# State space layer over quads of tokens: two groups on the halves of the array, tables made in the preceding block, states as stationary operand

## The reference

```
    lb_re, lb_im = mag * jnp.cos(ang), mag * jnp.sin(ang)          # one complex factor per group and state
    bb_re = cr[..., None] * b_re - ci[..., None] * b_im
    bb_im = cr[..., None] * b_im + ci[..., None] * b_re
    bu_re = jnp.einsum('blgh,gph->blgp', u, bb_re)
    bu_im = jnp.einsum('blgh,gph->blgp', u, bb_im)
    ...
    _, _, s_re, s_im = lax.associative_scan(combine, (a_re, a_im, bu_re, bu_im), axis=1)
    y = (jnp.einsum('ghp,blgp->blgh', c_re, s_re) - jnp.einsum('ghp,blgp->blgh', c_im, s_im)
         + d_skip.reshape(S5_GROUPS, S5_GROUP) * u)
    y = jax.nn.gelu(y.reshape(b_, L, D_MODEL), approximate=False)
    val, gate = jnp.split(y @ w_glu, 2, axis=-1)
    return val * jax.nn.sigmoid(gate)
```

## Time and profile before

| | us |
|---|---|
| median of 3 runs | 3628.16 |
| lowest and highest | 3626.93, 3628.58 |
| span of the profiled execution | 3628.5 |
| PE busy in it | 3462.6 |
| DVE busy | 2325.0 |
| ACT busy | 1840.1 |
| POOL busy | 509.8 |

### The profile page before, as it was taken

How to read it: one execution, slowest core, us unless ns; L and a number is a source line. 1 busy time by engine, 2 the same in 40 slices (tenths; PEclk the granted TensorE clock), 3 DMA queues, 4 the chain that set the end, 5 groups by cost and what they waited for, 6 DMA issues and landing times.

```text
span 3628.5 us, 63324 instructions
## 1 busy us (share of the span) xinstructions
PE 3462.6 (95%) x21770; PEld 3025.4 (83%) x21770; DVE 2325.0 (64%) x3755; ACT 1840.1 (51%) x2784; POOL 509.8 (14%) x546
## 2 busy tenths in 40 slices
PE   9997999999999999989999999999479999999998
PEld 7885888888888888878888888888468788888887
DVE  5687665555555766775765565778975665565566
ACT  4477454545454655544554454554554554454443
POOL 0001310111114000214000001133022000000105
PEclk9998999999999999999999999998589999999999
DMA  6561545555555555535455555652035455555555
GB/s 213 169 191 41 185 156 189 185 192 185 190 185 191 168 189 170 161 120 167 148 189 187 183 190 192 197 191 95 25 111 186 139 196 191 185 188 188 185 186 190
DMA packets 176036, 615.99 MB, mean 170 GB/s; under 512 B 19030, under 2 KB 28312, under 8 KB 175656
## 3 DMA queue, kind: packets, MB, share of 16 engines
q1 hardware_dynamic: 173212, 609.35, 51.9%
q10 hardware_dynamic: 2700, 4.96, 0.5%
HBM read 611.35 MB, written 2.88 MB: 169 GB/s over the span
## 4 chain that ended last, share of the span: by engine, by line
PE 88%; DVE 8%; ACT 2%; issue 1%; DMA 1%; SPq 0%; POOL 0%; ACTq 0%; DVEq 0%; POOLq 0%
PE bank L1881 53%; PE bank L1884 28%; PE m L1904 2%; DVE prod L1664 1%; DVE w_lo L1012 1%; DVE st L1667 1%; DVE st L1669 1%; PE m L1906 1%; PE m L1894 1%; ACT w_hi L433 0%; DVE y L1039 0%; PE m L2396 0%; PE bank L2396 0%; PE m L2297 0%; DVE res L1045 0%
## 5 line engine op out<-in xcount | busy, mean ns | idle before, releaser
L1012 DVE TENSOR_TENSOR w_lo<-w_raw,w_hi 128x1024 fp32r<-128x1024 f32 x1086 | 1336.2, 1252 | 815.6 <-ACT w_hi L433 809.6
L1881 PE MATMUL bank<-act,w_hi 128*128 128x512 f32 x6016 | 1512.6, 393 | 8.6 <-DVE w_lo L1012 7.9
L433 ACT ACTIVATE w_hi<-w_raw 128x1024 fp32r<-128x1024 f32 x1090 | 1130.1, 1055 | 389.8 <-PE bank L1884 348.9
L1881 PEld LDWEIGHTS bank<-act,w_hi 128*128 128x128 f32 x6016 | 1082.3, 189 | 209.0 <-DVE w_lo L1012 8.9
L1884 PEld LDWEIGHTS bank<-act,w_lo 128*128 128x128 f32 x6016 | 821.4, 191 | 58.9
L1884 PE MATMUL bank<-act,w_lo 128*128 128x256 f32 x6016 | 839.4, 282 | 0.0
L1881 PE MATMUL bank<-ffn,w_hi 128*128 128x512 f32 x2432 | 613.6, 393 | 1.3 <-DVE w_lo L1016 1.0
L442 ACT ACTIVATE low<-bank 128x256 f32<-128x256 f32 x542 | 207.9, 384 | 781.5 <-PE bank L1884 780.7
L1881 PEld LDWEIGHTS bank<-ffn,w_hi 128*128 128x128 f32 x2432 | 436.3, 189 | 79.5 <-DVE w_lo L1016 1.2
L1020 DVE TENSOR_TENSOR ev<-bank,low 128x256 f32<-128x256 f32 x468 | 198.3, 424 | 249.5 <-ACT low L442 243.5
L1884 PEld LDWEIGHTS bank<-ffn,w_lo 128*128 128x128 f32 x2432 | 333.9, 190 | 25.2
(11 more groups left out here) (412 smaller groups left out, 2490.3 us busy)
## 6 DMA issues: line engine op xcount, KB each, us to landing
w_raw<-stream SPq DMA_DIRECT2D x1148, 512.0 KB, 3.4
bias<-toeplitz SPq DMA_DIRECT2D x4, 512.0 KB, 9.0
out<-res SPq DMA_DIRECT2D x3, 512.0 KB, 2.9
res<-x_t SPq DMA_DIRECT2D x2, 512.0 KB, 9.0
res<-x_t ACTq DMA_DIRECT2D x2, 512.0 KB, 11.0
bias<-toeplitz SPq DMA_DIRECT2D x4, 256.0 KB, 11.8
b_raw<-s_b ACTq DMA_DIRECT2D x1, 1024.0 KB, 5.4
c_raw<-s_c ACTq DMA_DIRECT2D x1, 1024.0 KB, 4.7
```

Source lines behind the costliest of these rows:

```text
L433: a(w_hi[:, q, :], w_raw[:, q, :], ACT.Copy).then_inc(hi_ready, 1)
L1012: e.tensor_tensor(w_lo[:, q, :], w_raw[:, q, :], w_hi[:, q, :].bitcast(F32), ALU.subtract).then_inc(lo_ready, 1)
L1881: mm(bank[w][:, 0:2 * n], w_hi[:, q, wt], x(h * hk + k, 0, 2 * n), start=(h == 0 and k == 0), stop=False)
```

## The change

The stage works on four tokens at a time (quads). In words:

- **Recurrence.** The state after every fourth token is kept: 62 steps instead of 127 for each half of the groups, by the factor's fourth power. The step is unchanged (three instructions of the same shapes), `SKEW` is 12.
- **Layout of u.** Of every group the 16 channels of four tokens stand on 64 partitions, two groups on the two halves of the array. ACT writes the gained residual to `u_own`; PE moves it to that layout by 64 products with a 0/1 matrix `placing` (K = 32, 128 columns of weights, 256 columns of tokens read at every fourth; float32), partly between the sums of squares; DVE scales eight 128x512 tiles from PSUM to `u_quad` by the reciprocal root, which is now 64 columns wide.
- **Inputs.** 256 matmuls of 64x64 weights and 64 columns, two at a time on opposite quarters of the array; 16 PSUM tiles, 14 copied by ACT, 2 by DVE.
- **Tables.** C times five powers (`cd`, 48 DVE steps over 128x640) behind the up and down units of group 1, B times four powers (`b_lhs`, 16 times two steps over 128x512 and two over 128x256) behind group 2, with 16 loads of B and 16 of the powers (256 KB each) that ACT issues. PE does 6 transposes in group 0 in place of 32 in group 2. The 256 products for the direct taps, L2371, go from before the norm to the time of the scan (L2407). The down phase of group 0 is now written out on all engines, on ACT and DVE group 1 too.
- **Direct taps.** `k_own` is copied out of PSUM on 16 rows a half; eight SBUF-to-SBUF DMAs from SP place it, shifted, in `k_rhs` (runs of at most 256 bytes, 6144 of them in six DMAs, and two DMAs of whole rows); 128 matmuls multiply it, during the scan.
- **States.** `turned` becomes the stationary operand, `cd` the moving one (256 matmuls of 64x64, 64 columns); `gelu`; then 128 more matmuls with the identity turn the result back, the last two of eight tiles inside `first_pair` of `glu`. The rows of `w_glu` are permuted to suit.
- **Weights of glu.** `st` is half as large, so `hi` and `lo` of the first `glu` pair stand before the scan, and SP loads the second pair then.

The diff, cut to its core:

```diff
-    SKEW = 16
+    SKEW = 12
+    QUADS = 64
+    BY_DVE = (5, 7)
...
+    SLOT_UP1, SLOT_DOWN1, SLOT_UP2, SLOT_DOWN2 = 16, 48, 64, 88
+    C_SLOTS = [16 + n if n < 24 else 43 + n - 24 if n < 29 else 48 + (n - 29) * 16 // 19 for n in range(48)]
+    B_SLOTS = [66 + 11 * k // 4 if k < 8 else 88 + 2 * (k - 8) for k in range(DT)]
...
+        for half in range(2):
+            for j in range(4):
+                src, to = slice(64 * half, 64 * half + 16), slice(64 * half + 16 * j, 64 * half + 16 * j + 16)
+                sp_eng.dma_start(k_rhs[to, :, 16 * j:64], k_own[src, :, 0:64 - 16 * j]).then_inc(sem("k_moved"), 16)
...
+            if step == 0:
+                chain(e.tensor_tensor(to, table(0), c_of(r), ALU.mult))
+            elif step == 1:
+                chain(e.tensor_tensor(c_part[:, :, :, :], table(1), c_of(1 - r), ALU.mult))
...
+            for n in range(8):
+                h, i = n // 4, n % 4
+                v.wait_ge(sem("u_placed"), n + 1)
+                e.tensor_tensor(u_quad[:, 32 * h + i:32 * h + 32:4, :], five[n][:, :].rearrange("p (k c) -> p k c", k=8),
+                                rstd_row[:, :].unsqueeze(1).to_broadcast([P, 8, 64]), ALU.mult).then_inc(sem("u_scaled"), 1)
+            g0 = PH["glu"][0]
+            for q in range(4):
+                lo(g0, q)
...
-            for c in range(1, 128 + SKEW):
+            steps_ = QUADS - 1
+            for c in range(1, steps_ + SKEW):
...
+            def place(h, quad, of, done):
+                for j in range(4):
+                    for i in of:
+                        src, k0 = slice(32 * i, 32 * i + 32), 8 * h + 4 * quad
+                        last = mm(five[4 * h + i][:, 256 * quad:256 * quad + 256], placing[src, P * j:P * j + P],
+                                  u_own[src, k0:k0 + 4, j:T:4], start=(j == 0), stop=(j == 3))
+            for k in range(DT):
+                if k % 4 == 0 and k:
+                    place((k - 4) // 8, (k - 4) // 4 % 2, range(4) if k <= 8 else (0, 1), k == 8)
+                last = mm(m[5][:, 0:T], ones[:, :], u5_sq[:, k, :], start=(k == 0), stop=(k == DT - 1))
+            last.then_inc(sum_spread, 1)
+            place(1, 1, (0, 1), True)
+            pe.wait_ge(root_taken, NORM["s5"] + 1)
+            for i in (2, 3):
+                for quad in range(2):
+                    place(1, quad, (i,), quad == 1)
...
+            def states(n):
+                for k in range(8):
+                    for r in range(2):
+                        for rows in half_rows:
+                            last = mm(five[n][rows, 64 * k:64 * k + 64], turned[n][rows, k, r, :],
+                                      cd[rows, r, 8 * n + k, 1:5, :].rearrange("p d f -> p (d f)"), start=False, stop=(k == 7 and r == 1))
...
+            def back(n):
+                pe.wait_ge(sem("y5_gelu"), 2 * n + 2)
+                for w in range(2):
+                    for p_ in range(4):
+                        for half, rows in enumerate(half_rows):
+                            last = mm(five[n][rows, 256 * w + 64 * p_:256 * w + 64 * p_ + 64], y5[n % 4][rows, w, p_, :],
+                                      ident[rows, 64 * half:64 * half + 64], start=True, stop=True)
```

More of the change, by code:

```diff
@@ new lines, in build @@
+    b_raw = at("b_raw", -15, [P, 2, 64, 16])
+    d_dia = at("d_dia", -7, [P, 64, 16])
+    k_own = at("k_own", 16, [P, 64, 64])
+    k_rhs = at("k_rhs", 32, [P, 64, 64])
+    turned = [at(f"turned{n}", 16 + 4 * n, [P, 8, 2, 64]) for n in range(8)]
+    y5 = [at(f"y5_{n}", A + 38 + 2 * n, [P, 2, 4, 64]) for n in range(4)]
+    prod = at("prod", 98, [P, 2, 2, 2, 32])
+    rms_quad, rstd_row = at("rms_quad", 100, [P, 4, 64]), at("rstd_row", 101, [P, 64])
+    rms_pick, rms_row = at("rms_pick", 102, [P, 4, 64]), at("rms_row", 101.5, [P, 64])
@@ L951, in _ @@
-            for n in range(16):
-                turn(0, n)
-            for n in range(2):
-                gelu(0, n)
-            for n in range(8):
-                turn(1, n)
-            gelu(1, 0)
-            glu_high(0)
-            turn(1, 15)
-            s.wait_ge(sem("st_turned"), 25)
-            s.wait_ge(sem("st_dve"), 7)
+            for k in range(DT):
+                s.wait_ge(*stream_ready("s5")(k))
+                a(u_own[:, k, :], res[:, k, :], ACT.Copy, scale=gain2(1, 0)(k))
+                a(u5_sq[:, k, :], res[:, k, :], ACT.Square).then_inc(squared, 1)
@@ new lines, in _, with turn @@
+            for n in range(8):
+                s.wait_ge(sem("k_mm"), n + 1)
+                for half in range(2):
+                    rows = slice(64 * half, 64 * half + 16)
+                    a(k_own[rows, 8 * n:8 * n + 8, :], five[n][rows, :].rearrange("p (k c) -> p k c", k=8), ACT.Copy).then_inc(sem("k_cp"), 1)
+            def turn(n, second):
+                s.wait_ge(scan_step[n // 4], 3 * (62 if second else 30))
+                c = slice(32 * second, 32 * second + 32)
+                a(turned[n][:, :, :, c], st[:, c, :, 8 * n:8 * n + 8].rearrange("p t r k -> p k r t"), ACT.Copy).then_inc(sem("st_turned"), 1)
@@ new lines, in _ @@
+            s.wait_ge(sem("k_moved"), 128)
+            for n in range(4):
+                turn(n, 0)
+            s.wait_ge(sem("k_mm"), 9)
+            for n in range(4, 8):
+                turn(n, 0)
+            for n in range(4):
+                turn(n, 1)
+            for b in (0, 4):
+                gelu(b)
+                gelu(b + 1)
+                glu_high(b)
+                gelu(b + 2)
+                glu_high(b + 1)
+                gelu(b + 3)
+                glu_high(b + 2)
+                glu_high(b + 3)
@@ new lines, in s5_slot @@
+            if u == 10:
+                times(27, 25, 11)
+                times(29, 27, 11)
+            if u == 11:
+                times(31, 29, 11)
+                times(33, 31, 11)
+            for n in range(48):
+                if u == C_SLOTS[n]:
+                    weigh_c(n // 6, n % 6)
+            for k in range(DT):
+                late = k >= 8
+                if u == B_SLOTS[k]:
+                    weigh_b(k, 0)
+                if u == B_SLOTS[k] + (0 if late else 1):
+                    weigh_b(k, 1)
+                if u == B_SLOTS[k] + (1 if late else 2):
+                    weigh_b(k, 2)
@@ L2443, in _ @@
-            for b in range(2):
-                inputs(b)
-            for b in range(2):
-                outputs(b)
-            gemm("glu", x_act, 16, act_tile("glu"), entered="glu")
+            half_rows = [slice(64 * half, 64 * half + 64) for half in range(2)]
+            def place(h, quad, of, done):
[4 more added lines that the diff above has]
+                                  u_own[src, k0:k0 + 4, j:T:4], start=(j == 0), stop=(j == 3))
+                        if done and j == 3:
+                            last.then_inc(sem("u_placed"), 1)
@@ new lines, in back @@
+            def back(n):
+                pe.wait_ge(sem("y5_gelu"), 2 * n + 2)
+                for w in range(2):
+                    for p_ in range(4):
+                        for half, rows in enumerate(half_rows):
+                            last = mm(five[n][rows, 256 * w + 64 * p_:256 * w + 64 * p_ + 64], y5[n % 4][rows, w, p_, :],
+                                      ident[rows, 64 * half:64 * half + 64], start=True, stop=True)
+                last.then_inc(sem("y5_back"), 1)
+            for n in range(4):
+                states(n)
@@ L2448, in _, with last_turns @@
+            for n in range(4):
+                back(n)
+            for n in range(4, 8):
+                states(n)
+            back(4)
+            back(5)
+            pe.wait_ge(act_ready, DT * ACTS["glu"] + 4)
+            def last_turns(k):
+                if k in (0, 2):
+                    back(6 + k // 2)
+            gemm("glu", x_act, 16, act_tile("glu"), entered="glu", between=last_turns)
             norm("post_s5")
```

593 lines of the change are left out of this document (254 added, 339 removed).

## The result

The changed kernel takes 3584.9 us (median of 4 runs, 3582.15 to 3587.41) against 3627.7 for the kernel before; the ratio is 0.9881, 95% interval 0.9869 to 0.9892. That is 43 us less where 62 were forecast. The time lies inside the range given (3552 to 3592), but in the part that was added for the rivals: it is 19 us above the point forecast, 10 above the 3575 to which the forecast's own mechanism went (a chance of 0.50), and 6 above the 3579 of the first rival.

The account below looks back on a forecast made before the run. PE bounds the kernel except in the S5 stage, a serial chain. Recurrence -66.2, head +3.7, tail +6.3 and ffn0 -6.2 give -62.4 us, from 3628.2 to 3565.8, said as 3566; range 3552 to 3592.

Parts of the forecast that it names:

- the forecast's own mechanism: Whole kernel: the summed prices hold, 3566 us, with clock and stalls alone moving it between 3552 and 3575; chance 0.50.
- the first rival: Placing products before the scan: reading every fourth element doubles their time on all 32 groups, +13.7 us, 3579; chance 0.25.
- if DVE's scan waits for inputs: Recurrence: sign of being wrong in kind; the second half's inputs, 8.6 us, were to fit in 10.1 before step 13.
- 24 x 0.43 = 10.2: Head, after the fourth square: 12 more squares and 12 groups of placing products at 0.43 us each, 10.2 us on PE.
- 16 products on one strip each, 6.8: Head, behind the sum of squares: the last 16 placing products, each on a single row strip, take PE 6.8 us.
- 3.6 us for a half clock: Head: allowance of 3.6 us because placing products on a quarter of the rows may drop PE's clock.
- uses each column for two passes: Placing products: argument that a float32 matmul's two passes per column may hide the cost of the strided read.
- 48 x 0.85 + 16 x 2.4: ffn0: table preparation puts 79 us on DVE, which has 78 us idle in 179 us of group 1 alone.
- rival 4: ffn0: DVE's work behind its units is not hidden; if all 79 us land on PE, 3645 us; chance 0.03.
- (2): 64x64 products do not bring PE's clock back: scan starts 10 us later, about +38 in all, 3604; chance 0.12.
- (3): Short DMAs into k_rhs take over 25 us, so turns and states wait: +5 to +25, 3581 in the middle; chance 0.08.
- (5): Recurrence: the step price doubles for lack of overlap, so the change does not do what it says; given no chance.

Follow-up runs that it names:

- e7_warm: Changed kernel plus 92 zero-adding 64x64 products between direct taps and states; glu's first pair ends at E + 26.3 (E: recurrence's end), 2.45 us sooner, single execution.
- e6_no_late_weighing: Changed kernel with only the first of four DVE weighing instructions for the last eight B tables; ffn0's first pair to sum 729.8 us against 735.1, single execution.
- e1_contig_reads: Changed kernel with placing products reading 64 neighbouring columns instead of every fourth (tokens in wrong order); 3574.1 us, ratio 0.9844 to the kernel before.
- e3_strips_together: Changed kernel with the last 24 placing products reordered into groups on four and two row strips, strided read kept; 3577.6 us, ratio 0.9855 to the kernel before.

## Why the forecast was right where it was, and where it was wrong

**The recurrence: right.** 66.2 us less was forecast, 65.0 came. The steps cost what they cost before, since instructions and shapes are the same. Of the 1.2 us that are missing, 0.9 are the wait at step 13, where I had counted the second half's inputs at a steady 0.117 us a couple and not the 0.8 and 2.4 us in which PE stands. I had named it as a sign of being wrong in kind "if DVE's scan waits for inputs"; it does wait, though the wait is short.

**PE's prices for the new shape: right.** Inputs, states and turning back went at 0.93, 1.87 and 0.93 us a tile at full clock, as worked out from two other shapes in the earlier trace rows; four tiles of states with the clock at 1.00 took 7.6 us in `e7_warm`, 4 x 1.87 = 7.5.

**The head: wrong, and it is the step "24 x 0.43 = 10.2" (and "16 products on one strip each, 6.8" behind it).** I priced a placing product like a square, by the earlier trace rows, although I had seen that its read strides, and gave the doubled price 0.25. The record took 0.45 in place of 0.21 us. From the residual, the sum of squares came at 24.3 us in place of 14.9 (three blocks of placing 6.6 more; the first squares 1.1 late; the last four 1.2 longer; 0.5 is spread), placing ended at 39.3 in place of 23.4 (6.5 more behind the sum), and the recurrence began at 49.2 in place of 35.6. The first rival had this mechanism, and its price of +13.7 us meets the 13.6 found.

Part of that is luck. Placing itself took 13.1 us more: behind the sum its records at 0.45 add up to 18.0 us, but the strips ran side by side for 3 of them (2517.1 to 2519.1 and 2522.7 to 2524.1), which no sum had. And my base held 3.6 us for a half clock under placing, whose price turned out not to change with the clock. Half clock cost 3.6 us all the same, in other places: 1.1 at the first squares, which ran at a clock of 0.50 after PE's wait for the residual, 1.2 at the last four, and 1.3 at the first inputs (9.9 us for these and the copy where 8.6 stood in the sum). Right was that products on a quarter of the rows let the clock fall; it had fallen even before, behind a block on two strips.

The right choice was open from the rows. ACT's strided copy in the earlier trace rows was the only row with a strided read and showed a price nearly double (1.10 us for 512 elements, where L734 of the kernel before copies 512 neighbours in 0.60); against it I had set an argument without a row ("uses each column for two passes"), and it should have weighed less.

**ffn0: right in kind, wrong in size.** "48 x 0.85 + 16 x 2.4" was hidden in the up phases and in group 1, as forecast: PE there follows ffn1 within 0.6 us. It was not hidden in the last down phase, where 1.5 us was left for stalls. There each weighing takes 3.2 us, not 2.4, because the low parts and the weighing instructions themselves are slower than in the earlier trace rows, and DVE needs 9.0 us per 8.4 of PE's. Some 5 us came up to the sum, as `e6_no_late_weighing` shows, the upper end of the 0 to 5 that stood in the text, and 3.6 up to the residual. The mechanism of rival 4 is real, then, in one phase out of four. Another 1.1 us came back where nothing was forecast, between the sum and the residual: the sum now waits for POOL at a point by which DVE has part of the norm's work behind it.

**Tail: right within 0.7 us at each mark.** States at E - 9.06 (forecast E - 9.0), glu at E + 14.8 (15.5), first pair at E + 28.8 (28.6), with 2.5 us of half clock in it, which `e7_warm` gave back. That the last meets to 0.2 is partly luck, since unchanged runs end it at E + 27.8 to 28.9.

**The rivals.** (2) fell: the clock was back at 1.00 some 3 to 5.5 us into each run of 64x64 products. (3) did not bite: 15.8 us against a limit of about 16.7; I had it at 10 with 3 to spare, so the chance of 0.08 was low for what was in fact a near miss. (5) fell.

## What to carry to other kernels

Before pricing a matmul by its shape, look at how its moving operand lies in memory: one element used in every 16 bytes doubled the price of a float32 matmul at full clock (and changed nothing at half clock), two did not, and the engine that writes the operand could sort it for nothing. Work "hidden behind" a busy engine must be counted against the period of each phase with the durations of that phase, not with its price elsewhere. And once one long serial part is cut, look at what PE does in the microseconds before its next critical stretch: a filler that keeps the clock was worth 1.5 to 2.6 us here.

## What the runs showed that was not expected

- Strided reads of float32 columns by PE: 0.21 us for 256 neighbouring columns, 0.225 at every second, 0.45 at every fourth, the last the same at 1.2 and at 2.4 GHz. Row strips that run side by side each keep this pace, without slowing one another.
- ACT writes 256 elements, each 256 bytes from the last, in 0.73 us in place of 0.51; the pair with the square behind it grows only from 0.73 to 0.84 us.
- Six DMAs of short runs (64 to 192 bytes) and two of whole rows within the SBUF, 1280 KB together: SP's issues are spread over 10 us (0.6 to 2.5 us each), and the last lands 15.8 us after the first could start:

```profile
L435 SPq DMA_DIRECT2D k_rhs<-k_own x8: 630/1351/2481, 2568.2 to 2578.5; - x8
```

- Small products (64x64, 64 columns) on opposite quarters bring the clock back. Products on one strip of 32 rows lose it, with either read (0.50 in the changed kernel, 0.53 at their end in `e1_contig_reads`). Products on two strips lost it with the strided read, after 3.7 us of them (the squares behind them ran at 0.61 on average, in `e3_strips_together` at 0.55), and kept it with the neighbouring read, in 1.9 us. Whether the read or the length decides was not tested.
- A gap of 1.3 to 3.0 us in a dense stream of small products, at the same instruction in every run, with no semaphore: PE goes on 2.2 to 2.4 us after a packet of a queue called "instruction" starts. Whether the loads in flight delay that packet stays open.
